# One block for the whole program, gated products in wide form, root sums inside weight units

## The reference

```python
for i in range(2):                                # first_block
    u = rmsnorm(h, norm_g[i]) @ w_in[i]           # conv parts, q, k, v, gates
    ya = layernorm(conv31(a_val * sigmoid(a_glu))); ya = silu(ya) * silu(a_z)
    yb = window_attention(q, k, v) * silu(b_z)
    h = h + concat(ya, yb) @ w_out[i]
    e = rmsnorm(p[i] @ w_pe[i], pe_g[i])
    h = h + e * sigmoid(h @ w_pg[i])              # the gated stage
x = rmsnorm(h, final_g)
proj = rmsnorm(x, attn_norm_g) @ w_in_2           # second_block
y = concat(rwkv7_mixer(...), mla_mixer(...))      # 16 heads of 64; 8 latent-attention heads
x = x + y @ w_out_2
g = causal_conv3(rmsnorm(x) @ w_gate) + b         # 5632 features
x = x + (silu(g) * (rmsnorm(x) @ w_up)) @ w_down
out = rmsnorm(x, final_norm_g)
```

## Time and profile before

| | us |
|---|---|
| median of 3 runs | 2329.83 |
| range of the runs | 2328.87 to 2333.64 |
| the profiled execution | 2330.22 |
| its span in the trace | 2328.4 |
| mean granted clock of TensorE | 0.985 of full |

### The profile page before, as it was taken

How to read it: one execution, slowest core, us unless ns; L and a number is a source line. 1 busy time by engine, 2 the same in 40 slices (tenths; PEclk the granted TensorE clock), 3 DMA queues, 4 the chain that set the end, 5 groups by cost and what they waited for, 6 DMA issues and landing times. The chain is left out here.

```text
span 2328.4 us, 40865 instructions
## 1 busy us (share of the span) xinstructions
PE 2250.9 (97%) x15552; PEld 2025.2 (87%) x15552; DVE 1726.2 (74%) x2935; ACT 1058.6 (45%) x1403; POOL 568.9 (24%) x226
## 2 busy tenths in 40 slices
PE   7999989999999989999999899999999999999997
PEld 5888988998888978999999788788888888888897
DVE  7688658885888478888878755778888886557876
ACT  5444454444444554545544622444444443333443
POOL 3766631017766520110000321110000000000014
PEclk9999999999999999999999989999999999999999
DMA  7454334555545344554445300255555555555554
GB/s 236 165 177 177 139 140 165 189 185 186 184 168 177 129 161 165 182 191 164 160 149 169 126 1 20 82 189 182 191 186 183 195 180 189 190 183 194 183 205 174
DMA packets 69036, 384.94 MB, mean 165 GB/s; under 512 B 15089, under 2 KB 22769, under 8 KB 23985
## 3 DMA queue, kind: packets, MB, share of 16 engines
q1 hardware_dynamic: 68912, 383.22, 46.8%
HBM read 380.02 MB, written 3.18 MB: 165 GB/s over the span
## 5 line engine op out<-in xcount | busy, mean ns | idle before, releaser
L258 PE MATMUL ps<-opA,whi 128*128 128x512 f32 x2100 | 746.1, 395 | 0.9 <-issue 0.9
L228 ACT ACTIVATE whi<-raw 128x2048 fp32r<-128x2048 f32 x346 | 660.1, 1908 | 112.3 <-DMA raw<-weights_dram 112.1
L233 DVE TENSOR_TENSOR low<-raw,whi 128x2048 fp32r<-128x2048 f32 x252 | 578.9, 2297 | 75.7 <-ACT whi L228 49.9
L259 PE MATMUL ps<-opA,low 128*128 128x256 f32 x2240 | 604.0, 280 | 0.0
L240 POOL TENSOR_TENSOR low<-raw,whi 128x2048 fp32r<-128x2048 f32 x95 | 437.0, 4612 | 456.3 <-ACT whi L228 431.4
L258 PEld LDWEIGHTS ps<-opA,whi 128*128 128x128 f32 x2100 | 394.7, 188 | 92.0 <-issue 3.5
L259 PEld LDWEIGHTS ps<-opA,low 128*128 128x128 f32 x2240 | 421.1, 188 | 11.8
L258 PE MATMUL ps<-opB,whi 128*128 128x512 f32 x1020 | 371.7, 403 | 18.2 <-DVE opB L401 11.6
L259 PE MATMUL ps<-opB,low 128*128 128x256 f32 x1088 | 296.5, 283 | 0.0
L267 ACT ACTIVATE crossed<-ps 128x256 f32<-128x256 f32 x152 | 58.4, 384 | 498.3 <-PE ps L261 498.3
L246 PE MATMUL ps<-opB,whi 128*128 128x256 f32 x944 | 272.3, 288 | 1.8 <-DVE opB L972 1.1
(11 more groups left out here) (400 smaller groups left out, 3641.9 us busy)
## 6 DMA issues: line engine op xcount, KB each, us to landing
raw<-weights_dram SPq DMA_DIRECT2D x350, 1024.0 KB, 4.8
bias_t<-table_dram SPq DMA_DIRECT2D x16, 384.0 KB, 6.0
hT<-xT_dram SPq DMA_DIRECT2D x4, 512.0 KB, 9.0
out_dram<-hT SPq DMA_DIRECT2D x4, 512.0 KB, 2.9
lora_g<-lora_dram SPq DMA_DIRECT2D x1, 1024.0 KB, 4.8
p_in<-pT_dram SPq DMA_DIRECT2D x2, 256.0 KB, 2.8
lora_wa<-lora_dram SPq DMA_DIRECT2D x1, 512.0 KB, 5.7
chunk_mats_dram<-compact SPq DMA_DIRECT2D x4, 128.0 KB, 4.0
```

Of the source, the lines that this page charges most:

```text
L228: act.activation(whi[:, v % RING, :], raw[:, v % RING, :], ACT.Copy).then_inc(hi_done.sem, 1)
L233: v_.tensor_tensor(wlo(v % RING, 0, width), raw[:, v % RING, 0:width], whi[:, v % RING, 0:width].bitcast(F32), ALU.subtract).then_inc(lo_d ...
L258: pe.matmul(*cross, start=start, stop=False)
L259: mm = pe.matmul(ps[:, b, 0:T], wlo(s, w0, w0 + P), op[:, k, 0:T], start=False, stop=False)
```

## The change

1. **One block.** `phase_mla` and `phase_within` become stages, and all stages run in one `together(...)`. In place of the barriers come waits: latent attention's PE waits for `phase_mix`'s last eviction, its POOL for its last unit, its DVE for the causal mask; in `phase_within` POOL waits for the last transposed output of latent attention, PE for the loaded solve matrices; in `phase_chain` SP's load of `lora_g` and ACT's first copies wait for `phase_within`.
2. **Opening.** POOL's first split waits for `x_sum`. The root sum stands before step 4 of the third unit, where it stood before step 12.
3. **Residual in place.** h is written to `hT` directly, the operand and the squares are made from it, and the copy L979 goes, except in down2.
4. **Gated stages wide.** A new `add_halves` on DVE (`tensor_reduce` over the two halves, into bank 4 or 5) stands ahead of the weight split, and tanh reads its result.
5. **Root sum of the mixed stages** inside the ninth unit, before step 8.
6. **Mix.** The root sums go inside the second unit, before step 6; the third unit writes to bank 4 without a wait for an eviction.
7. **down2** is wide, with `act_cross` and the addition L1074.

```diff
@@ def act_cross
+        def add_halves(v, b, to):
+            return v.tensor_reduce(to, ps[:, b, :].rearrange("p (h t) -> p t h", h=2), axis=AX.X, op=ALU.add)
-        def pe_unit(pe, u0, j, i, op, ..., order=None, free=False):
+        def pe_unit(pe, u0, j, i, op, ..., order=None, free=False, within=None):
...
             for n, k in enumerate(order or range(kb)):
+                if within is not None and n == within[0]:
+                    within[1]()
@@ phase_front
             def _(pool):
+                if l == 0:
+                    pool.wait_ge(*x_sum(1))
                 pool.wait_ge(lo_done.sem, u0 + LEAD + ahead)
...
-                        if k == 12:
+                        if k == 4:
                             pe.wait_ge(*x_sum(1))
                             stat_pe(pe, stat)
@@ residual_step
-            v.tensor_tensor(t3[:, 0:T], hT[:, c, :], add, ALU.add).then_inc(new.sem, 1)
+            v.tensor_tensor(h, h, add, ALU.add).then_inc(new.sem, 1)
...
-                link(v.tensor_scalar(hT[:, c, :], t3[:, 0:T], 1.0, None, ALU.mult))
@@ phase_residual
-                        act.wait_ge(mm_done.sem, 4 * i + (u0 + j + 1))
-                        act.activation(t1[:, 0:T], ps[:, (u0 + j) % 2, 0:T], ACT.Tanh, scale=0.5).then_inc(ev_done.sem, 1)
+                        act.wait_ge(added.sem, added.base + 4 * i + j + 1)
+                        act.activation(t1[:, 0:T], ps[:, 4 + (u0 + j) % 2, 0:T], ACT.Tanh, scale=0.5).then_inc(ev_done.sem, 1)
...
+                        if gated:
+                            v.wait_ge(mm_done.sem, 4 * i + (u + 1))
...
+                            add_halves(v, u % 2, ps[:, 4 + u % 2, 0:T]).then_inc(added.sem, 1)
                         dve_split(v, u0, j, i)
...
                     units(pe, u0, 8, body, head=4)
-                    pe.wait_ge(*e_summed(KB))
-                    stat_pe(pe, stat)
-                    units(pe, u0 + 8, 8, lambda j, i, m: body(j + 8, i, m + 8))
+                    body(8, 0, 8, (8, root_sum))
+                    units(pe, u0 + 9, 7, lambda j, i, m: body(j + 9, i, m + 9))
@@ phase_mix
-                    pe_unit(pe, u0, j, 0, op, ready=ready if j == 0 else None)
-                    if j == 0:
-                        pe.wait_ge(*summed(KB))
...
+                    pe_unit(pe, u0, j, 0, op, ready=ready if j == 0 else None, bank=bank_of(j), free=j == 2, within=(6, root_sums) if j == 1 else None)
@@ phase_within
-            with nc.Block() as block:
-                @block.gpsimd
+            @stage.gpsimd
                 def _(pool):
+                pool.wait_ge(*ml["outT"](MLA_H))
@@ program
-        together(*stages, phase_mix(u, opnd[1], ready, summed))
+        stages += [phase_mix(u, opnd[1], ready, summed)]
...
-        phase_mla()
-        phase_within(u)
+        stages += [phase_mla(u), phase_within(u)]
...
-        together(chain, normed, mixed, up, down, up2, down2, phase_out(down2.summed))
+        together(*stages, chain, normed, mixed, up, down, up2, down2, phase_out(down2.summed))
```

More of the change, by code:

```diff
@@ L267, in act_cross, with pe_unit @@
             act.activation(crossed[:, b, :], ps[:, b if bank is None else bank, T:2 * T], ACT.Copy).then_inc(read.sem, 1)
[L269 removed]
+        def add_halves(v, b, to):
+            return v.tensor_reduce(to, ps[:, b, :].rearrange("p (h t) -> p t h", h=2), axis=AX.X, op=ALU.add)
+        def pe_unit(pe, u0, j, i, op, kb=KB, k0=0, start=True, stop=True, bank=None, need=1, ready=None, wide=False, order=None, free=False, within=None):
             u = u0 + j
@@ L997, in phase_residual @@
             head = 4 if ready is not None else 0
-            read = cross_read.ahead(KB) if wide else None
+            read = cross_read.ahead(KB) if wide and not gated else None
+            added = halves_added.ahead(KB) if wide and gated else None
             stage = Stage()
@@ L1011, in body @@
                         act_split(act, u0, j, i)
-                    if wide and (j + 1) % per_block == 0:
+                    if wide and not gated and (j + 1) % per_block == 0:
                         act_cross(act, u0, j, i, ((u0 + j) // per_block + flip) % 2, read, early[m] if opened else None)
@@ L1080, in body @@
                             v.memset(small[:, 1:2], 0.0).then_inc(ev_done.sem, per_block)
-                steps = (2 if nxt is not None else 1) + (1 if gated or wide else 0)
+                steps = (1 if nxt is not None or gain is not None else 0) + (1 if gated or wide else 0)
                 if e_gain is not None:
@@ new lines, in phase_mla, with _ @@
+            stage = Stage()
+            @stage.gpsimd
+            def _(pool):
+                pool.wait_ge(mm_done.sem, u_next)
+                pool.memset(lower[:, 16:32, :], 0.0).then_inc(mx["cleared"].sem, 1)
+            @stage.sync
+            def _(sp):
+                sp.wait_ge(*mx["cleared"](1))
+                for c in range(4):
+                    sp.dma_start(lower[32 * c:32 * c + 32, :, 32 * c:32 * c + 32],
+                                 chunk_mats[32 * c:32 * c + 32, :, :].rearrange("i s t -> s i t")).then_inc(mx["sol_in"].sem, 16)
@@ L1935, in phase_within, with _ @@
-            for n, s in wi.items():
-                s.passed({"mn": 32, "mn_read": 32, "ends": RW_B}.get(n, 16))
+            stage = Stage()
+            @stage.gpsimd
+            def _(pool):
+                pool.wait_ge(*ml["outT"](MLA_H))
+                for pair in range(RW_B):
+                    factor = spread(pc[:, pair, :], CH, 2).rearrange("p (s c) t -> p s c t", s=2)
+                    for x, src in enumerate((a_gate, k_)):
+                        ins = pool.tensor_tensor(chunk_ends[:, pair, :, x, :].rearrange("p s (c t) -> p s c t", t=CH),
+                                                 src[:, pair, :].rearrange("p (s c t) -> p s c t", s=2, t=CH), factor, ALU.mult)
+                    ins.then_inc(wi["ends"].sem, 1)
+                for j in range(LEAD):
+                    pool_split(pool, u_next - LEAD, j)
@@ L1937, in program @@
+            return stage
         held = place("held", [P, 4, DH], at=word_rows)
@@ L2229, in program @@
             gated = phase_residual(u, opnd[cur], opnd[1 - cur], in2_gain if last else par_of("norm_g", l + 1), gated=True,
-                                   squares=1 + last, ready=mixed.written)
+                                   squares=1 + last, ready=mixed.written, wide=True)
             u += 16
```

448 lines of the change are left out of this document (221 added, 227 removed).

## The result

| | before | changed |
|---|---|---|
| median, us | 2331.73 (4 runs) | 2308.2 (4 runs) |
| range, us | 2328.87 to 2335.1 | 2307.67 to 2313.62 |
| profiled execution, us | 2330.22 | 2307.67 |
| span, us | 2328.4 | 2305.9 |

The ratio is 0.9904 (95% interval 0.9882 to 0.9925): 23.5 us faster, where 28 were forecast. The time lies inside the stated range and above the forecast's own value of 2302 by 6 us.

A forecast was written before the change was run, and what follows sets the result against it. PE, busy 97% of the span, was taken as the bound, leaving waits, the half clock behind them and the wide step to win. -6.9 - 11.0 - 4.8 - 3.0 - 0.85 - 1.0 = -27.6 gave 2302 us, range 2291 to 2314.

The forecast's parts named there:

- the root sums: Mixed stages: root sum inside the ninth unit removes the wait and half clock, -6.1 and -4.9, together -11.0 us.
- A: Opening: with POOL held back, x_sum comes early and the seventh unit starts at 50.4 instead of 57.27, -6.9 us.
- C: Gated stages wide: units of 5.61 us instead of 5.76, reduction 0.68 us, over 32 units -4.8 us.
- D: Start of mix: old waits go, a new 1.6 us wait for DVE at the fourth unit, -3.0 us.
- Residual in place costs and gives nothing elsewhere: Residual written directly to hT: priced at nothing elsewhere, as PE does not wait for DVE in the mixed stages.
- E: One block: shorter waits at the within-chunk stage (-0.65) and the start of latent attention (-0.2), -0.85 us.
- F: down2 wide: -1.9 us for shorter steps, +0.9 at the very end, -1.0 us.
- The first: Rival, within-chunk stage: the 17 us half-clock stretch from 1340 to 1357 goes too, -9 more, 2293 us; 25%.
- The second: Rival, gated stages: reduction takes 1.1 to 1.2 us, DVE bounds at a 6.0 us cycle, 2314.5 us; 15%.
- The third: Rival, opening: splits collide with DVE again or the seventh load lands late, gain there only -4, 2305 us; 6%.
- The fourth: Rival, gated stages: reduction 1.8 us or more, PE waits over 1 us a unit and clock halves, 2355 us; 2%.
- if PE has new stretches at the lower clock: Sign on PE's timeline that would show the prediction wrong; the other was a gated-stage DVE cycle over 5.76 us.

The follow-up runs named there:

- the second execution: The changed kernel, unaltered, timed and traced once more: 2307.03 us, ratio to the kernel before 0.9898.
- loads first: Changed kernel with SP requesting the next weight unit before the embedding inputs and bias tables in the front stages: 2305.23 us, ratio to the kernel before 0.9894.
- Gated narrow: Changed kernel with the gated stages narrow again (three matmuls of 256 columns, no reduction), residual in place kept: 2311.28 us, ratio to the kernel before 0.9918.
- the best version: Changed kernel with weight loads requested first and the within-chunk copy of held step matrices moved from DVE to ACT: 2298.23 us, ratio to the kernel before 0.9854.

## Why the prediction held, and where it was off

**Direction and size.** The forecast of -27.6 us came out as -22.5 in the trace and -23.5 in the medians. Part of that nearness is luck: the gains that nobody forecast, -3.1 at the end of mix and -1.3 more at its start, cover 4.4 of the 9.5 us by which the other places came out short. The terms for the gated step (0.15 us a unit, a reduction of 0.68 that took 0.70) and for the root sums (-11.0 against -9.9) were right in mechanism. The second was too large by 0.6 us a place: the step "a wait of some 0.2 us stays, with the matmul 0.3" counted the root matmul at 0.12 us, and with the slow step behind it it costs 0.7.

**A, mis-sized: -6.9 against -4.** The step "its load is issued when the third unit is done", at 32.8, was wrong: the request came at 35.41. One us of this is the half-clock stretch from 17 us; the second execution, without it, has -5.0. Another us is SP's queue: SP had a table round trip, the embedding's input and two bias transfers ahead of it, so the request came 1.4 us after the unit's last matmul started, where with loads first it comes 0.4 after. The 11.0 us from request to use came out as 11.2, and that wait of the load kept PE standing for 2 us. But the 11.0 is not the load's own time, as the row that shows it also has the bias transfers ahead: requested first, the load is in use after 6.4 us.

**C, a consequence missed: +1.8.** The prediction knew that the last operand part would come 5.4 us after the last gated unit and used it for PE's sixteenth step only. The same semaphore holds SP in the next front stage. Gated narrow and loads first each remove the stall, so this is shown twice.

**D, mis-sized and wrongly credited.** The gain is 4.3 and the new wait 0.22 us, where 3.0 and 1.6 were forecast; DVE's series ended at +19.0 instead of +19.5, and PE came to the fourth unit at +18.9 instead of +17.9, since small products for the decay stand ahead of it that the sum left out. More important, the prediction put it down to moving the sums and the spare bank; undoing these costs 1.3 us. The other 3 are the wait for the last operand and the half clock behind it, which go because DVE comes in time.

**"Residual in place costs and gives nothing elsewhere"** is the step that failed most. Taking it away (in the gated stages and the second block's mixed stage) costs 21 us. The prediction had counted the missing copy in C's cycle without saying that the whole term hung on it: with the copy DVE's cycle is 5.8 us in the first layer and 6.4 to 6.9 in the second, over PE's 5.61, and DVE is late for mix. Of the edits that were undone one at a time, the one whose loss costs most is the one that was priced at nothing. Even without the copy the margin is thin: in the first layer DVE waits only 0.10 to 0.19 us for PE ahead of most reductions, 0.67 in the second.

**E and F.** The waits at the stage starts fell by 0.28 and 0.68 us as predicted. The traces still show +0.5 from latent attention to the chain, not -0.85: the within-chunk stage took 103.0 us from its first mask to the chain, where it had been 98.9, with 20.5 us at half clock instead of 17.1 and a new wait of 1.30 us for DVE. F was forecast at -1.0 and is nil: behind the last unit stand not only ACT's copy and DVE's addition (0.9), but 0.5 us in which DVE waits for POOL's square of the unit before, as the square's ACT work now stands behind the cross copy, and 0.5 us by which the root sum is slower at half clock.

**The rivals.** The first (the long half-clock stretch goes) did not come: the stage has 20.5 us at half clock in the changed kernel's profile and 7 to 41 in those of the experiments. Its cause is partly another than I thought, DVE's copy behind POOL. The second did not come, the reduction being 0.70; its price rule was right. The third is what happened in the opening: the seventh load was late, and A is the -4 that it named; what made it late is the queue and the clock. The fourth's condition, a wait over 1 us in each unit, was made and its price refuted; its sum was also off, as a third of 32 units at 5.6 us is 60 us, not 53.

**The signs.** One sign of being wrong that the prediction gave, "if PE has new stretches at the lower clock", did come: the changed kernel has one from 17 us and one of 13.7 us in the within-chunk stage. It was a bad sign, as such stretches differ between executions of one kernel. And "the waits are few" left out the two of 4.08 us for ACT's copy, which was no error in the sum, since no edit touches them.

**What stays open.** The -3.1 us at the end of mix: 0.7 less waiting, and a stretch of 3.4 us at half clock, at 1265 us before, that is missing in nine of the thirteen traces of changed kernels and present in four. Whether an edit makes it rarer was not tested. Nor was the residual in place with narrow gated stages, nor what sets the length of a half-clock stretch.

## What to carry to other kernels

When a change lengthens the tail of a stage on one engine, follow its last semaphore to every engine that waits for it, the queue of transfers among them: a small transfer that waits holds every weight load behind it. An instruction that is removed from the engine with the second-fullest cycle may be what makes another edit possible, so price it with the other edit in place and without. And compare stages between traces, not totals: here one trace of the best version was slower than the median of the version it improves.

## What the hardware showed that was not expected

- A copy of 128x256 from SBUF to SBUF on DVE takes 0.29 us, and 3.66 to 7.51 us when it starts beside POOL's subtraction of 128x2048, ending within 0.2 us of POOL's end. DVE's short operations that read PSUM in the same stretch keep their 0.22 to 0.29 us. The Trainium skill names this in GPSIMD Engine Reference, Specifications: contention with VectorE instructions in a two-port mode or with two SBUF inputs. The trace agrees, and the prediction, which had cited it, had looked only at instructions with two inputs. Moving the copy to ACT removed the wait.
- Standing 1.25 us in every 7.1 us did not lower TensorE's granted clock (1.00 over 60 us), while single waits of 1.3 to 3 us elsewhere were followed by 3.4, 6.8, 13.7 or 34 us at half clock, and by different lengths at the same place in different executions of the same work.
- A weight load of 1 MB requested ahead of two bias transfers was in use at most 6.4 us later, behind them 11.2 us later.
